# RMS norm of a two-layer decoder step moved behind its projections

## What is computed

```python
def rmsnorm(x, g):
    y = x * rsqrt(mean(x * x, -1) + EPS)
    return y * g
for l in range(2):
    z = rmsnorm(x, norm1_g[l]) @ w_in[l]          # q, k, v, gates, pooling input, ...
    mq, mk, mv, mi, mf, mo, gq, gk, gv, glr, go, pu, gates = split_cols(z)
    y_ml   = head_rmsnorm(mlstm(mq, mk, mv, mi, mf)) * sigmoid(mo)
    y_gla  = head_rmsnorm(gla(gq, gk, gv, glr)) * silu(go)
    y_pool = pool_mixer(pu)
    x = x + sum(sigmoid(gates) * (branches @ w_branch)) @ w_out
    h = rmsnorm(x, norm2_g[l])
    if l == 0: x = x + (silu(h @ wg) * (h @ wu)) @ wd
    else:      x = x + top-2-of-8 experts of that form, chosen by softmax(h @ router_w)
y = rmsnorm(x, final_norm_g)
```

## Time and profile before

| what | value |
|---|---|
| median of 3 runs | 2482.98 us (2480.99 to 2484.28) |
| the profiled execution, its own time | 2478.01 us |
| its span, first to last instruction | 2476.3 us |
| PE busy | 2235.2 us, 90% |
| DVE busy | 1227.6 us, 50% |
| ACT busy | 941.7 us, 38% |
| POOL busy | 441.4 us, 18% |
| TensorE clock granted, mean of the span | 0.941 of full |

### The profile page before, as it was taken

The page is one execution under the profiler, slowest core; times in us unless marked ns, Lnnn a source line. Parts: engine busy times, 40 slices in busy tenths (PEclk is TensorE's granted clock), DMA queues, the critical chain, the costliest instruction groups (busy, mean ns, idle before and its releaser), DMA issues.

```text
span 2476.3 us, 39023 instructions
## 1 busy us (share of the span) xinstructions
PE 2235.2 (90%) x15763; PEld 2044.0 (83%) x15763; DVE 1227.6 (50%) x1718; ACT 941.7 (38%) x1258; POOL 441.4 (18%) x387
## 2 busy tenths in 40 slices
PE   6999999749899999989999997598699999999994
PEld 6999887539899999989998875398588888887883
DVE  3225433655343332232254336553377777677775
ACT  3224333141333322132244231413355555555556
POOL 0000212131000000000002121310233443444343
PEclk9999999769999999999999997699699999999996
DMA  4323422325523332323234223251377777776775
GB/s 141 93 86 99 148 75 84 111 87 167 228 79 91 93 94 86 92 64 93 86 99 148 79 79 117 86 164 60 123 223 236 225 230 227 235 233 225 236 226 173
DMA packets 102634, 341.70 MB, mean 138 GB/s; under 512 B 13128, under 2 KB 17256, under 8 KB 102248
## 3 DMA queue, kind: packets, MB, share of 16 engines
q1 hardware_dynamic: 85416, 278.46, 36.3%
q0 software_dynamic: 15568, 56.34, 6.8%
q10 hardware_dynamic: 1536, 5.24, 0.6%
HBM read 294.28 MB, written 46.17 MB: 137 GB/s over the span
## 4 chain that ended last, share of the span: by engine, by line
PE 61%; issue 18%; POOL 10%; DVE 5%; ACT 4%; DMA 1%; POOLq 0%; SPq 0%; ACTq 0%; DVEq 0%
PE ps L1574 49%; PE ps L1568 9%; POOL w_lo L643 9%; DVE h_lo L1045 1%; DVE sq L1040 1%; POOL br_lo L612 0%; DMA ifb<-if_bias 0%; POOL token_slots L658 0%; ACT mixed L851 0%; ACT L805 0%; ACT wgt L805 0%; DVE Cs L1262 0%; DVE num L1267 0%; DVE Cq L1264 0%; ACT w_hi L685 0%
## 5 line engine op out<-in xcount | busy, mean ns | idle before, releaser
L685 ACT ACTIVATE w_hi<-raw 128x1024 fp32r<-128x1024 f32 x488 | 514.0, 1055 | 569.3 <-PE ps L1574 492.6
L1025 DVE TENSOR_TENSOR w_lo<-raw,w_hi 128x1024 fp32r<-128x1024 f32 x383 | 473.1, 1235 | 380.9 <-ACT w_hi L685 377.5
L1574 PE MATMUL ps<-h_hi,w_hi 128*128 128x260 f32 x2800 | 587.8, 292 | 34.2 <-DVE h_lo L1045 26.0
L1574 PE MATMUL ps<-h_hi,w_lo 128*128 128x260 f32 x2800 | 573.5, 287 | 0.0
L1574 PE MATMUL ps<-h_lo,w_hi 128*128 128x260 f32 x2800 | 572.9, 287 | 0.0
L1574 PEld LDWEIGHTS ps<-h_hi,w_hi 128*128 128x128 f32 x2800 | 442.4, 193 | 56.1 <-issue 46.9
L1574 PEld LDWEIGHTS ps<-h_hi,w_lo 128*128 128x128 f32 x2800 | 441.5, 193 | 0.0
L1574 PEld LDWEIGHTS ps<-h_lo,w_hi 128*128 128x128 f32 x2800 | 440.9, 193 | 0.0
L1883 PE MATMUL ps<-hg,w_hi 128*128 128x320 f32 x1408 | 378.1, 351 | 27.7 <-POOL w_lo L643 25.4
L1885 PE MATMUL ps<-hg,w_lo 128*128 128x160 f32 x1408 | 337.3, 240 | 0.0
L643 POOL TENSOR_TENSOR w_lo<-raw,w_hi 128x1024 fp32r<-128x1024 f32 x105 | 250.2, 2387 | 397.2 <-ACT w_hi L685 397.0
(11 more groups left out here) (336 smaller groups left out, 2724.6 us busy)
## 6 DMA issues: line engine op xcount, KB each, us to landing
raw<-slabs SPq DMA_DIRECT2D x489, 512.0 KB, 3.9
gates_kept<-sq SPq DMA_DIRECT2D x64, 260.0 KB, 2.1
gs<-gates_kept POOLq DMA_DIRECT2D x64, 260.0 KB, 3.2
token_slots<-zeros POOLq DMA_DIRECT2D x1, 9600.0 KB, 34.7
rows_in<-token_slots POOLq DMA_DIRECT2D x9, 512.0 KB, 5.6
Cs<-ml_C POOLq DMA_DIRECT2D x8, 512.0 KB, 4.1
C_s<-Cs POOLq DMA_DIRECT2D x8, 512.0 KB, 2.9
token_slots<-yt ACTq DMA_DIRECT2D x8, 512.0 KB, 2.7
```

The lines of the kernel that those rows point to most:

```text
L685: nc.scalar.activation(w_hi[:, n % SPL], raw[:, place(n)], ACT.Copy).then_inc(hi_ready, 1)
L1025: tt_op(w_lo[:, n % SPL], raw[:, place(n)], w_hi[:, n % SPL].bitcast(F32), ALU.subtract).then_inc(lo_ready, 1)
L1574: ins = mm(out[:, hf], wgt_part[:, slot, tile], in_part[:, kk, HALF * hf:HALF * (hf + 1)], start=first and not ends and in_part is in_hi, ...
```

## The change

- **Input of the projections.** `h_hi` and `h_lo` are the parts of x times the norm's gain, without the root (`gained_hi` on ACT, `gained_lo` on DVE). They are made tile by tile in the stage that makes x: while the output projection, or the down projection, adds to x.
- **Squares.** `square` (ACT) and `add_square` (DVE) follow in the same place and sum the squares of the tiles in `rs[:, 1]`. PE's `mean_squares` is then 2 matmuls in place of 16, and stands behind the first slab (behind the second in layer 0), not ahead of it.
- **The root on the outputs.** Each output of `inputs` is multiplied by the root `rs[:, 0]`, all of it on DVE now. A gate is multiplied by the root on DVE first (`gate_scale`) and gets its sigmoid after it, on ACT, out of `sq`. In the feed-forward DVE does two more multiplications a tile.
- **Mixed.** It has buffers of its own, `mixed_hi` and `mixed_lo`, and is split a pair of tiles at a time during the merge.
- **Router.** The logits are ranked without the root; a column of roots per token (`token_squares`, `rs_col`) scales logits and rows; the rows that go to the experts are x's rows times root times a gain row (`h_row`), the gain row being spread by two more matmuls in the output projection of layer 1.
- **Start.** SP loads the norm gains first, then half of x, slab 0, the other half, slab 1, and only then the constants.
- The feed-forward's first turn of 12 slabs is written out ahead of PE's loop.

The core of the diff (declarations, renamed semaphores and the routing's table steps left out):

```diff
-        sp.dma_start(con[:], consts).then_inc(loaded, 16)
-        for i in range(2):
-            half = slice(i * KT // 2, (i + 1) * KT // 2)
-            sp.dma_start(x[:, half], x_in[:, half]).then_inc(x_in_half[i], 16)
-        sp.dma_start(vec[:], vectors).then_inc(loaded, 16)
-        sp.dma_start(ifb[:], if_bias).then_inc(loaded, 16)
+        sp.dma_start(vec[:], vectors).then_inc(vectors_in, 16)
...
+        for i in range(2):
+            half = slice(i * KT // 2, (i + 1) * KT // 2)
+            sp.dma_start(x[:, half], x_in[:, half]).then_inc(x_in_half[i], 16)
+            load(i)
+        sp.dma_start(con[:], consts).then_inc(loaded, 16)
+        sp.dma_start(ifb[:], if_bias).then_inc(loaded, 16)
+        for n in range(2, turns_from):
...
+        def gained_hi(r, kk, ready):
+            act.wait_ge(*ready)
+            nc.scalar.activation(h_hi[:, kk], x[:, kk], ACT.Copy,
+                                 scale=gain_of(r)[:, kk:kk + 1]).then_inc(h_hi_ready, 1)
+        def square(r, kk):
+            i = 8 * r + kk
+            if i >= 2:
+                act.wait_ge(squares_used, i - 1)
+            nc.scalar.activation(sq[:, kk % 2], x[:, kk], ACT.Square).then_inc(squared, 1)
+        def norm(r):
+            act.wait_ge(ssq_ready, r + 1)
...
+            o = l * O_LAYER1 + Z_MO + i
+            act.wait_ge(gate_scaled, l * N_GATES + i + 1)
+            if H <= i < 2 * H:
+                if i > H:
+                    act.wait_ge(*evac(o - 1))
+                nc.scalar.activation(rs[:, 1], sq[:, i % 2], ACT.Sigmoid).then_inc(gate_sig, 1)
+            else:
+                nc.scalar.activation(sq[:, i % 2], sq[:, i % 2], ACT.Sigmoid).then_inc(emptied[o % 2], 1)
...
+            def mixed_high(mp):
+                act.wait_ge(mix_steps, 16 * l + 4 * (mp + 1))
+                for kk in (2 * mp, 2 * mp + 1):
+                    nc.scalar.activation(mixed_hi[:, kk], mixed[:, kk], ACT.Copy).then_inc(
+                        mixed_hi_ready, 1)
...
+                if s in (4, 7, 10):
+                    mixed_high(s // 3 - 1)
+            mixed_high(KT // 2 - 1)
             for m in range(KT):
                 split_hi(nb + S_OUT + m + 2)
+                gained_hi(2 * l + 1, m, evac(ob + O_OUT + m))
+                square(2 * l + 1, m)
...
+        def gained_lo(r, kk):
+            dve.wait_ge(h_hi_ready, 8 * r + kk + 1)
+            stt_op(h_lo[:, kk], x[:, kk], gain_of(r)[:, kk:kk + 1], h_hi[:, kk].bitcast(F32), ALU.mult,
+                   ALU.subtract).then_inc(h_lo_ready, 1)
+        def add_square(r, kk):
+            dve.wait_ge(squared, 8 * r + kk + 1)
+            if kk == 0:
+                ins = nc.vector.tensor_copy(rs[:, 1], sq[:, 0])
+            else:
+                dve.wait_ge(squares_used, 8 * r + kk)
+                ins = tt_op(rs[:, 1], rs[:, 1], sq[:, kk % 2], ALU.add)
+            ins.then_inc(squares_used, 1)
...
+                if i > 0:
+                    gate_scale(fills[1], i - 1)
+        def gate_scale(l, i):
+            n, o = l * LAYER1 + Z_MO + i, l * O_LAYER1 + Z_MO + i
+            if H < i <= 2 * H:
+                before = o - 1
+                dve.wait_ge(gate_sig, H * l + i - H)
+                tt_op(sq[:, (i - 1) % 2], sq[:, (i - 1) % 2], rs[:, 1], ALU.mult).then_inc(
+                    emptied[before % 2], 1)
+            out_done(n)
+            if i >= 2:
+                dve.wait_ge(*gate_kept(l, i - 2))
+            tt_op(halves(sq[:, i % 2]), out_ps(o), halves(rs[:, 0]), ALU.mult).then_inc(gate_scaled, 1)
...
+        def mixed_low(l, mp):
+            for kk in (2 * mp, 2 * mp + 1):
+                dve.wait_ge(mixed_hi_ready, 8 * l + kk + 1)
+                tt_op(mixed_lo[:, kk], mixed[:, kk], mixed_hi[:, kk].bitcast(F32),
+                      ALU.subtract).then_inc(mixed_lo_ready, 1)
...
+                dve.wait_ge(slab_done, j * FF_TURN + (nf + 2 * t + 1))
+                tt_op(halves(af[:, t % 2]), out_ps(o), halves(rs[:, 0]), ALU.mult).then_inc(act_scaled, 1)
+                dve.wait_ge(act_scaled, f)
+                tt_op(rs[:, 1], af[:, t % 2], rs[:, 0], ALU.mult).then_inc(emptied[o % 2], 1)
                 split_lo(nf + 2 * t + 3, j)
+                dve.wait_ge(*evac(o, j))
                 dve.wait_ge(sig_ready, f)
-                tt_op(halves(af[:, t % 2]), out_ps(o), halves(sig[:]), ALU.mult).then_inc(
-                    emptied[o % 2], 1)
-                dve.wait_ge(*evac(o, j))
+                tt_op(rs[:, 1], rs[:, 1], sig[:], ALU.mult).then_inc(gate_done, 1)
+                dve.wait_ge(gate_done, f)
...
+        def h_row(i):
+            rws = slice(0, tile_rows(i))
+            dve.wait_ge(x_rows_ready, i + 1)
+            stt_op(first[rws, i], xt[rws, i], rs_col[rws, i:i + 1], gain_row[rws], ALU.mult,
+                   ALU.mult).then_inc(h_rows_ready, 1)
...
+        def mean_squares(r):
+            pe.wait_ge(squares_used, 8 * (r + 1))
+            for hf in range(2):
+                ins = exact(ps[:, 4 + hf, 0:HALF], ones, rs[:, 1, HALF * hf:HALF * (hf + 1)])
+            ins.then_inc(ssq_ready, 1)
...
+        def token_squares():
+            pe.wait_ge(squares_used, 32)
+            for i in range(5):
+                rws = tile_rows(i)
+                ins = exact(ps[0:rws, 3, i:i + 1], rs[:, 1, P * i:P * i + rws], ones[:, 0:1])
+            ins.then_inc(ssq_ready, 1)
...
+                if l == 1 and m == 1:
+                    pe.wait_ge(gain_diag_ready, 1)
+                    for hf in range(2):
+                        ins = exact(ps[:, 6 + hf], ones, rows_in[:, 0, 512 * hf:512 * (hf + 1)])
+                    ins.then_inc(gain_row_ps, 1)
...
+            for i in range(FF_TURN):
+                slab_to_out(nf + i, of + i, h_hi, h_lo, None if i else (h_lo_ready, 1))
+                if i == 0:
+                    mean_squares(1)
+            with pe.Fori(1, FF_TURNS) as j:
...
+                if i == 1 - l:
+                    pe.wait_ge(loaded, 32)
+                    mean_squares(2 * l)
...
-        def mean_squares(r, bank_free):
-            for s, n in bank_free:
-                pe.wait_ge(s, n)
-            for kk in range(KT):
-                pe.wait_ge(squared, 8 * r + kk + 1)
-                for hf in range(2):
-                    ins = exact(ps[:, 4 + hf, 0:HALF], ones, sq[:, kk % 2, HALF * hf:HALF * (hf + 1)],
-                                kk == 0, kk == KT - 1)
-                ins.then_inc(squares_used, 1)
```

More of the change, by code:

```diff
@@ L286, in decoder @@
     mix.close()
+    merged = ExitStack()
+    mixed_hi = sb("mixed_hi", [P, KT, T], F32R, where=merged)
+    sb("between", [P, 36 - KT, T], where=merged)
+    mixed_lo = sb("mixed_lo", [P, KT, T], F32R, where=merged)
+    merged.close()
     ffn = ExitStack()
@@ L721, in inputs @@
                 split_hi(n + 2)
[L722 to L725, removed]
+                if i == 0:
+                    norm(2 * l)
+                    act.wait_ge(loaded, 32)
+                    act.wait_ge(small_scaled, 2 * (l + 1))
+                    nc.scalar.activation(row_i[:], row_i[:], ACT.Identity,
                                          bias=ifb[:, l, 0:1]).then_inc(rows.sem, 1)
-                    nc.scalar.activation(halves(row_f[:]), src[32:32 + H], ACT.Identity,
+                    nc.scalar.activation(row_f[:], row_f[:], ACT.Identity,
                                          bias=ifb[:, l, 1:2]).then_inc(rows.sem, 1)
[L729 to L735, removed]
         def gla(l):
@@ L910, in feed_forward @@
             hidden_tiles(nf, of, FF_TURNS, FF_REST)
+            m = 0
             for s in range(F_TILES):
                 split_hi(nf + S_DOWN + s + 2)
+                while m < KT and (F_TILES * (m + 1) - 1) // 8 == s:
+                    gained_hi(2, m, evac(of + O_DOWN + m))
+                    square(2, m)
+                    m += 1
         def gathered_hi(p, b):
@@ L924, in turned @@
             nc.scalar.activation(to[0:rws, i].rearrange("p (a d) -> p a d", a=2),
-                                 ps[0:rws, pair(at + i):pair(at + i) + 2], ACT.Copy).then_inc(ready, 1)
+                                 ps[0:rws, pair(i):pair(i) + 2], ACT.Copy).then_inc(ready, 1)
         def routing():
@@ L986, in _ @@
         fills = [0, 0]
[L987 removed]
+        act.wait_ge(vectors_in, 16)
+        split_hi(0)
+        for kk in range(KT):
+            gained_hi(0, kk, (x_in_half[kk // 4], 16))
+        split_hi(1)
+        act.wait_ge(loaded, 32)
+        for kk in range(KT):
+            square(0, kk)
         for l in range(DEPTH):
             nb, ob = l * LAYER1, l * O_LAYER1
[L990 removed]
             inputs(l, nb, ob)
@@ L1029, in out_done @@
             dve.wait_ge(slab_done, n + 1)
[L1031 to L1042, removed]
-                    dve.wait_ge(h_hi_ready, 8 * hs + kk)
-                    own = hf[:, kk - 1] if r == 3 else sq[:, (kk - 1) % 2]
-                    tt_op(h_lo[:, kk - 1], own, h_hi[:, kk - 1].bitcast(F32),
```

(3 more changed lines are left out.)

195 lines of the change are left out of this document (106 added, 89 removed).

## The result

The changed kernel takes 2519.8 us (median of 4 runs, 2515.8 to 2523.1) against 2483.6 before: a ratio of 1.0154, 95% interval 1.0142 to 1.0166. It is slower, as forecast, but by 36 us where I had forecast 14.5, and it lies 1.8 us above the range.

A forecast was written before the change was run, and what follows sets the result against it. PE was taken as the bound, busy 2235 of 2476 us, so only changes to its waits count. Gains -67.2, new waits +65.6 and clock +16 gave +14.4 on 2483.0: 2497.5 us, range 2466 to 2518.

The forecast's parts named there:

- norms, merge, start: Waits removed at both layers' norms, the router, the merges and the kernel's start: together 67.2 us gained.
- a product's wait in a chunk: GLA chunks: a half slab waits for the silu gate's product, 2.9 us idle, 8.8 in 3 chunks.
- gate 9, first decode half: GLA decode: the fourth silu product comes late behind DVE's `w_lo`, and PE waits 4.8 us.
- gate 14, row vectors, more than before: Row vectors: gate 14's slab waits for gate 12's later sigmoid, 4.0 us.
- heads 1 and 3, `wcol`, each more: Heads 1 and 3: a sigmoid starting later delays the exponentials up to `wcol`, and PE loses 2.1 us each.
- head 0, `wcol`: Head 0: the later exponentials up to `wcol` cost PE 0.6 us.
- GLA's start, layer 0 and layer 1: Gate 1's later sigmoid delays exponentials and `qz`: PE's first chunk starts 2.3 us late, in layer 1 3.7.
- decode and head norm, a layer: Last pool output waits 1.3 us; last gate, scaled behind the fourth decode head, costs at least 1.3: 2.6 together.
- The clock: Half speed for 3.4 us behind the mixers' new or longer gaps: 8 us a layer, 16 in all, between 0 and 34.
- No clock loss: Rival: gains 67.2 against waits 65.6 with no half-speed cost, 2481.5 us, no change; chance 0.12.
- Slack takes the ACT delays: Rival: only the silu products cost time (27 us), other waits absorb late sigmoids: 2443 us, faster; chance 0.19.
- POOL's contention: Rival: scalings and products in the heads stretch beside POOL, some 14 us in both layers, more clock losses: 2515; chance 0.15.

The follow-up runs named there:

- experiment 6: Changed kernel with 22, 22, 22 and 36 matmuls nobody reads filling PE's gaps at gates 6 to 9 of each layer: 2504.1 us, ratio 1.0094.
- Experiment 8: experiment 7 with each layer's last gate scaled and put through its sigmoid right after the last gate slab: 2441.6 us, ratio 0.9842.
- experiment 4: Changed kernel with VectorE doing a silu gate's product ahead of its turn's weight split, not behind it: 2503.9 us, ratio 1.0091.
- experiment 7: experiment 3 with ScalarE issuing a gate's sigmoid one gate later: 2446.7 us, ratio 0.9865.
- experiment 3: Changed kernel with a gate's PSUM output declared free by the scaling, not by the following sigmoid or product: 2473.7 us, ratio 0.9984.

## Why the prediction was wrong in size

**What held.** The sign and its reason: the norms' gaps are given back where gates are filling. By its steps, us of both layers where not said:

| step | forecast | measured |
|---|---|---|
| norms, merge, start | -67.2 | -64.0 |
| a product's wait in a chunk | 2.95 | 3.01, six times |
| gate 9, first decode half | 4.8 | 4.86, twice |
| gate 14, row vectors, more than before | 4.0 | 4.2 (5.21 less 1.02) |
| heads 1 and 3, `wcol`, each more | 2.1 | 2.05 (4.73 less 2.68) |
| gates behind the pool product, each | 1.3 | 1.36 |
| head 0, `wcol` | 0.6 | 2.1 |
| GLA's start, layer 0 and layer 1 | 2.3 and 3.7 | 1.5 and 1.4 |
| decode and head norm, a layer | 2.6 | 5.65 and 5.46 |
| all waits of the mixers | 65.6 | 72.6 |
| half speed | 16 | 33.1 |

**The step that failed is "The clock".** I had taken half speed for 3.4 us behind 3 in 4 of the gaps of 2.9 and behind those near 5, 8 us a layer and 34 at most. In the decode heads PE idles every few microseconds and stays at 1.2 GHz for 44 us (41 before). Outside that run the trace after has ten gaps of 2.1 to 5.2 us in each layer's mixers; 19 of these 20 are followed, or ended, by a stretch at 1.2 GHz. I had counted six a layer and not the heads' gaps of 2.1 and 2.3 (the decode's of 3.9 was 2.1 before and had its stretch then too), I had let a quarter of the gaps of 2.9 go free, and five of the stretches last 6.8 us and not 3.4. The one behind the first decode half, and layer 1's first gap in the chunks, which alone had none behind it:
```profile
262.45:269.20 6.75, 5.76 (x26) 5.79 (x27) 2.68 (x4) 0.64 (x1) 0.00 (x0) 0.50 0.84 294
1288.60:1291.50 2.90, 0.00 (x0) 0.00 (x0) 2.90 (x6) 0.00 (x0) 0.00 (x0) 1.00 0.00 0
1291.60:1295.00 3.40, 3.40 (x29) 3.40 (x30) 0.43 (x1) 0.64 (x1) 0.00 (x0) 1.00 0.70 230
```
Of the 27.3 us by which the forecast of the difference (14.4) missed the traces' 41.7, this term makes 17.1, the waits 7.0 and the gains 3.2. (A count of stretches gives only the rough size. The 14 of 3.4 and 5 of 6.8 us behind gaps are 81.6 us, at half speed 40.8 lost. But five more stand behind no gap of over 1 us, three of 3.4 and two of 6.8, and the kernel before had nine of 3.4 outside the decode heads, of which four behind gaps of 2.1 to 2.7. All of them make a difference of 37 us; PE idled in a part of that time.) That busy time grew by the clock and not by other matmuls is shown by the number of records, 3041 in both kernels in layer 1, and by experiment 6 in the chunk stages.

**The waits' 7.0** are two mis-sized terms, 5.9 (decode and head norm) and 3.0 (head 0), and 1.2 in small parts of others, less 3.1 by which the GLA's start was idle for less than forecast. For the head norm I had written "1.3 at least": the last gate's chain was ended by its store, which ScalarE waits for before it may square. The answering rows of the changed kernel, ScalarE with the store's issue on the DMA queue between:
```profile
547.93 0.64 ACT L875 ACTIVATE sq<-sq 128x520 f32<-128x520 f32 x1 [39.66 <-DVE sq L1341]
551.92 1.16 ACT L841 ACTIVATE sq<-br 128x520 f32<-128x520 f32 x2 [3.35 <-DMA gates_kept<-sq]
```
```profile
548.59 0.33 SPq L494 DMA_DIRECT2D gates_kept<-sq  x1
```
Scaling, sigmoid and then 3.35 us for the store: PE waits 7.48 where it waited 2.96, 4.5 more. Experiment 8 shows that this chain is the cause: begun earlier, it leaves a wait of 2.95. For head 0 I had counted on slack that the changed kernel doesn't have: it waits 2.1 in both layers. In experiment 4's layer 0, where half speed fell just ahead of it (301 to 308), it waits 0.58; slack and clock trade.

**The gains** fell 3.2 short. At the start slab 0 begins at 13.8 where my estimate was 11.7, and the third slab at 32.7, not 31.6: 1.2 less than forecast. (It comes 13.5 us earlier than before, and the half speed behind the gap of 5.06 takes back 2.2, which I had allowed for.)
```profile
13.80 0.77 PE L1675 MATMUL ps<-h_hi,w_hi 128*128 128x260 f32 x2 [13.80 <-DVE h_lo L1068]
```
From the experts' first matmul to the end of the span it is 1.7 us more than before, 0.7 are missing in the merge and the router, and the stage between the layers' mixers gave 0.4 more than forecast. In the working itself, the terms for the feed-forward's third slab add up to 14.3 us behind the last `x`, not to the 14.6 written there; measured were 14.4.

**The rivals.** "No clock loss" is wrong by 33 us. "Slack takes the ACT delays": the heads' exponentials came 2.05 later and PE's wait grew by just that; no slack, as experiment 7 confirms from the other side. "POOL's contention": none of the 64 scalings took longer than 0.70 us, though 15 of them ran beside an instruction of POOL:
```profile
L1341 DVE TENSOR_TENSOR sq<-ps,rs x64: 679/693/700, 182.4 to 1615.6; 128x520 f32<-128x520 f32 x64
```
The Trainium skill, "GPSIMD Engine Reference", section "1. Specifications", names VectorE's instructions with two SBUF inputs, or in a mode with two ports, as those that contend; a scaling has one SBUF input, and this trace agrees. The Trainium skill, "TensorE: Matmul & The Clock Gate", section "HAM oscillation — how this bites in real kernels", puts the return to half rate down to long waits for data. The trace doesn't agree that only long waits count: nine of the ten waits of 2.1 to 3.0 us were followed by it, as all ten of 3.9 to 5.2 were, and the measurement decides.

## What to carry to other kernels

When normalization moves from a matmul's input to its output, the output's buffer gets a longer tail (a scaling, then what used to be first). Let the buffer be declared free by the last instruction that reads it and nothing behind; here that one semaphore was worth 42 to 46 of the 105.7 us that the mixers had lost. Then look at what else stands in the queue of each engine that now waits for another: an activation that never had to wait is a stop for all behind it, and one turn's delay of its issue takes it away (27 us more). And price a new wait of TensorE of some 2 to 5 us at its length plus the half speed behind it, counted for every such gap: in this kernel that added almost half to the waits.

## What the runs showed of the hardware

Half speed behind a gap is not one size. The same gap of 3.01 us was followed by 3.4 us at 1.2 GHz four times, by 6.8 once and by none once; gaps of 1.87 by half speed in four of six places, gaps of 1.84 in another kernel in one of six, and gaps of 1.36 in the changed kernel in none of four. In the kernel before two of the four gaps of 2.68 had it, and five stretches stood behind no gap of over 1 us. What decides between these I could not tell from the traces. When the gaps were filled with matmuls, no such stretch was left in the chunk stages of either layer.

Taking away some waits moved half speed to other places: with the products' waits gone (experiment 3), the row vectors' stage of layer 0 ran at a clock of 0.88 and not 0.94, though its wait was shorter. So the clock's share can't be split over single waits, only over a stage or the kernel.
